# Delta-rule stage of a two-block model: two chains over tile pairs become four chains over single tiles

## The chip, the cores and the metric

The kernel runs on one NeuronCore of one Trainium2 chip. The metric is the device time of one execution in microseconds (us). Three executions of the kernel before took 3952.75, 3956.01 and 3965.37 us; the median is 3956.01 us. The engines are TensorE (PE; its weight loads are shown apart as PEld), VectorE (DVE), ScalarE (ACT), GpSimd (POOL) and SyncE (SP), which issues the DMAs.

## The reference, cut to what matters

The reference is a block of mixers and experts followed by a second block. Only one piece of it is touched here, the RWKV-7 scan of the first block. For each of 8 heads of width 64, for each of two directions of time (forward and reverse), over 256 context tokens and then 1024 latent tokens:

```python
def step(s, inp):
    r_t, w_t, k_t, v_t, a_t, b_t = inp
    sa = einsum('bhvk,bhk->bhv', s, a_t)
    s = s * w_t[:, :, None, :] + sa[..., None] * b_t[:, :, None, :] + v_t[..., None] * k_t[:, :, None, :]
    y = einsum('bhvk,bhk->bhv', s, r_t) if emit else None
```

The outputs of both directions are added, normalized over each head's 64 values (mean, variance, square root), scaled and shifted by `lnx_g` and `lnx_b`, and then `(yn + bonus) * gate` goes to the array `mix`. Everything is float32.

## The kernel before

The kernel is a row of stages with a barrier between them: modulation, the first projection (`project_first`), `rwkv_mix`, `hgrn_mix`, the experts, the second block. Between the barriers each engine runs its own list of instructions in order; semaphores order the engines among themselves. Only `rwkv_mix` (L972 to L1480) is changed, and with it the layout of the arrays in DRAM that it reads.

The stage works in chunks of 64 tokens. Inside one chunk the scan becomes linear algebra: with the products of the keys and queries of the chunk, masked to what comes before (`at`, `cb`, `bkT`, `ck`), one needs the inverse of a unit triangular 64x64 matrix. It is built by doubling: `T` and its transpose `TT` start from blocks of two, and five levels (`w1`, `t1` ... `w5`, `t5`) double the block size. A level multiplies a masked copy `X` of `at` with `T` (step `w`, and VectorE adds the identity to give `W`), and then `TT` with `W` (step `t`, which gives the new `T`). One such problem is a chunk of one head in one direction: 20 chunks x 8 heads x 2 directions = 320 problems. Each is a 64x64 matrix, so four matmuls can stand in the four quadrants (64 rows x 64 columns) of the 128x128 array.

Two chains (`u` = 0, 1) go side by side. Each owns four banks of PSUM. A unit of a chain is one group of 128 channels (two heads) and two tiles of 128 tokens, in both directions: 16 problems. A chain makes 10 units, 5 for its first group of channels and 5 for its second; the 20 units of both chains make the stage. A unit is cut into steps:

- `turn`: 16 transposes of a, b, k and v (L1185); the copies go to ACT (L1298) and DVE (L1353).
- `prodb`, `prodk`: products of b and k with a and r (L1199), which DVE masks (L1346).
- `zed`: masked product with v (L1211). `t0`: `T` from `TT` by products with the identity (L1162).
- POOL makes the first `TT` by three masked multiplications and the addition of the identity (L1445, L1456), and the five `X` (L1441).
- `w` and `t` (L1162): each level also makes the turned inverse `TT` by 16 matmuls of its own, copied by DVE (L1370, L1374).
- `wup` (L1172): inverse times a and times the masked values; `mn` (L1237, L1243, L1244): per chunk a matrix `m` and an addend `n`, so that the state goes through four short steps `c0` to `c3` (L1269, L1399), each `S = m S * tot + n`.
- `intra`, `query`, `inter` (L1252, L1253, L1260, L1280): the outputs, added up in `yacc` (L1409), of both directions.
- After a group's fifth unit the whole of `yacc` (128x1024) is normalized: `mean`, `square`, `var`, `root`, `norm`, `back`, `gate` (L1416 to L1432, L1319, L1323, L1286, L1328, L1474, L1476), and stored (L1143).

The order on each engine is written out by one loop (`interleaved`): for each round `s`, for each chain `u`, it emits the step number `s - OFFSET*u` of that chain, with `OFFSET` 11. An engine that waits for one chain's step holds back the steps of the others that stand behind it in its list.

SP loads a unit two units ahead (L1129 to L1132, 12 DMAs for a unit). Before its first work ACT waits for the two small loads of `lnx` (semaphore `once`, L1118 and L1119, the first DMAs of the stage).

## Time and profile before

| | us |
|---|---|
| median of three runs | 3956.01 |
| span of the profiled execution | 3941.6 |
| median less that span (before the first and after the last instruction, and run to run) | 14.4 |
| first DMA of the stage changed, from the span's start | 771.72 |
| first DMA of the next stage | 1358.74 |
| the stage changed | 587.0 |
| PE busy in it | 441.89 |
| DVE, ACT, POOL busy in it | 316.05, 135.19, 224.26 |

Busy time of a matmul includes the time in which it runs through the array, so a busy PE is not PE at its peak. A group with a small mean can be many short instructions at close distance. The distance from the start of one instruction to the start of the next says more of an engine's rate than the duration of one. The mean granted clock of TensorE was 0.933 over the span. The page's own chain of waits reaches back only to 3743.91 us, into the last projection; it says nothing of the stage changed.

### The profile page before, as it was taken

The numbers are of one execution on the slowest core, as the hardware profiler recorded it, in microseconds if no ns is written. First come the engines' busy times: TensorE is split into PE (matmuls) and PEld (weight loads), VectorE is DVE, ScalarE is ACT, GpSimd is POOL, SyncE is SP. The second block draws the span as 40 slices with busy tenths as digits, with TensorE's granted clock in tenths as the row PEclk, the third lists the DMA queues.
The fourth block names the chain that finished last, engine by engine and source line by source line (L and its number), as shares of the span: only waits on it lengthen the run. The fifth ranks groups of instructions, "written<-read, shape, count | busy, mean of one in ns | idle before, by whom it ended". The sixth has DMA issues, their size and how long they took to land. (4 is left out here: it accounts for less than half of the span.)

```text
span 3941.6 us, 97846 instructions
## 1 busy us (share of the span) xinstructions
PE 3377.2 (86%) x38463; PEld 2331.6 (59%) x38463; DVE 2360.6 (60%) x4245; ACT 1768.8 (45%) x2361; POOL 731.1 (19%) x706
## 2 busy tenths in 40 slices
PE   4999799677778587979998998999689999878789
PEld 0899788577677475733332333333267777666567
DVE  1688688655555466627776766776377574056631
ACT  0577577422222124307776766776222321156620
POOL 4000000043444200331221221222112333200000
PEclk7999899899899788989999999999899999988899
DMA  8354445421221255949889999953734323265452
GB/s 315 84 171 139 160 130 166 159 86 46 61 72 44 82 167 200 209 155 315 277 263 356 351 354 357 326 160 76 244 87 128 86 75 96 95 153 132 117 181 75
DMA packets 520291, 665.36 MB, mean 169 GB/s; under 512 B 77168, under 2 KB 423984, under 8 KB 516768
## 3 DMA queue, kind: packets, MB, share of 16 engines
q1 hardware_dynamic: 494576, 572.44, 45.2%
q0 software_dynamic: 25216, 86.62, 8.9%
q8 instruction: 312, 5.11, 0.5%
q14 instruction: 139, 1.14, 0.1%
q10 hardware_dynamic: 48, 0.05, 0.0%
HBM read 493.08 MB, written 165.94 MB: 167 GB/s over the span
## 5 line engine op out<-in xcount | busy, mean ns | idle before, releaser
L2600 PE MATMUL routed_p_gu<-routed_fixed,routed_x 128*32 128x512 f32 x3840 | 572.5, 600 | 0.0
L2600 PE MATMUL routed_p_gu<-moe_exp_w,routed_x 128*32 x1280 | 571.5, 600 | 0.7 <-DVE routed_fixed L2722 0.7
L2654 ACT COPY routed_fixed<-moe_exp_w 128x1024 f32 x320 | 332.6, 1047 | 222.1 <-DMA moe_exp_w<-in_exp_w_up_dram 86.3
L2722 DVE COPY routed_fixed<-moe_exp_w 128x1024 f32 x640 | 398.0, 681 | 51.3 <-DMA moe_exp_w<-in_exp_w_up_dram 42.9
L544 PE MATMUL front_ps<-front_a_high,front_w_high 128*128 128x320 f32 (+1 forms) x1120 | 362.7, 324 | 16.3 <-DVE front_w_low L797 13.4
L544 PE MATMUL front_ps<-front_a_low,front_w_high 128*128 128x320 f32 (+1 forms) x1120 | 353.8, 316 | 0.0
L544 PE MATMUL front_ps<-front_a_high,front_w_low 128*128 128x320 f32 (+1 forms) x1120 | 353.7, 316 | 0.0
L2600 PEld LDWEIGHTS routed_p_gu<-moe_exp_w,routed_x 128*32 128x32 f32 x1280 | 135.4, 111 | 356.2 <-issue 356.2
L3606 PE MATMUL pre_ps<-pre_a_high,pre_w_high 128*128 128x512 f32 x720 | 287.1, 399 | 13.3 <-ACT pre_xb L3753 6.7
L2615 PE MATMUL routed_p_y<-routed_wd,routed_hT 128*32 x640 | 290.4, 597 | 3.4 <-ACT routed_fixed L2665 3.4
L2615 PE MATMUL routed_p_y<-routed_fixed,routed_hT 128*32 128x512 f32 x1920 | 291.4, 597 | 0.0
L2734 DVE COPY routed_fixed<-routed_wd 128x1024 f32 x320 | 201.7, 691 | 141.2 <-PE routed_p_gu L2600 126.8
L3606 PE MATMUL pre_ps<-pre_a_high,pre_w_low 128*128 128x512 f32 x720 | 281.3, 391 | 0.0
L3606 PE MATMUL pre_ps<-pre_a_low,pre_w_high 128*128 128x512 f32 x720 | 281.2, 391 | 0.0
L2557 POOL DMA_INDIRECT total<-rw_mask,routed_yidx x80 | 128.6, 1608 | 732.2 <-ACT rw_mask L2671 604.6
L544 PEld LDWEIGHTS front_ps<-front_a_high,front_w_high 128*128 128x128 f32 x1120 | 213.3, 190 | 35.2 <-DVE front_w_low L797 18.0
L1445 POOL TENSOR_TENSOR rwmix_TT<-rwmix_at,rw_mask 64x256 f32<-64x256 f32 (+1 forms) x60 | 43.5, 725 | 922.4 <-DVE rwmix_at L1346 916.5
L544 PEld LDWEIGHTS front_ps<-front_a_low,front_w_high 128*128 128x128 f32 x1120 | 213.2, 190 | 1.3
L544 PEld LDWEIGHTS front_ps<-front_a_high,front_w_low 128*128 128x128 f32 x1120 | 213.0, 190 | 0.0
L2665 ACT COPY routed_fixed<-routed_wd 128x1024 f32 x160 | 167.1, 1047 | 47.4 <-PE routed_p_gu L2600 46.7
L2615 PEld LDWEIGHTS routed_p_y<-routed_wd,routed_hT 128*32 128x32 f32 x640 | 70.8, 111 | 196.9 <-issue 196.9
L3606 PEld LDWEIGHTS pre_ps<-pre_a_high,pre_w_high 128*128 128x128 f32 x720 | 135.9, 189 | 46.7 <-issue 16.5
(550 smaller groups left out, 7386.6 us busy)
## 6 DMA issues: line engine op xcount, KB each, us to landing
moe_exp_w<-in_exp_w_gate_dram SPq DMA_DIRECT2D x64, 1024.0 KB, 13.3
moe_exp_w<-in_exp_w_up_dram SPq DMA_DIRECT2D x64, 1024.0 KB, 16.4
routed_wd<-in_exp_w_down_dram SPq DMA_DIRECT2D x64, 1024.0 KB, 15.1
front_wt<-in_w_in_dram SPq DMA_DIRECT2D x70, 512.0 KB, 4.4
mod_w<-in_w_mod_dram SPq DMA_DIRECT2D x24, 1024.0 KB, 18.2
pre_wt<-in_w_in_dram SPq DMA_DIRECT2D x44, 512.0 KB, 4.0
out_a<-mix SPq DMA_DIRECT2D x24, 512.0 KB, 4.0
total<-out_none SPq DMA_DIRECT2D x24, 512.0 KB
```

Source lines behind the costliest of these rows:

```text
L544: op = nc.tensor.matmul(ps[:, s % 2, c, 0:size], w_part[:, s % 2, k, :], a_part[:, k, first + c * size:first + (c + 1) * size], start=(k = ...
L1445: nc.gpsimd.tensor_tensor(combos(TT[u][:])[to, es], combos(at[u][:])[at_rows, es], mask(MASK_LEVEL, at_rows, es), ALU.mult)
L2557: nc.gpsimd.indirect_dma_start(total, bass.IndirectOffsetOnAxis(ap=yidx[b % 2][:, :], axis=0), y[:, b % 2, :], None, compute_op=ALU.add).t ...
L2600: op = nc.tensor.matmul(p_gu[spot(s), :], x[:, b % 2, k, spot(s)], w, start=(k == 0), stop=(k == KD - 1))
L2615: op = nc.tensor.matmul(p_y[spot(s), h, :], hT[:, m, spot(s)], w, start=(m == 0), stop=(m == MT - 1))
L2654: nc.scalar.copy(fixed[:, place_of(b, c), 0, :], wgu[:, bass.ds(e % WS, 1), c * D:(c + 1) * D].rearrange("p o n -> p (o n)"))\
L2665: nc.scalar.copy(fixed[:, at, 0, :], wd[:, bass.ds(e % WD, 1), m, :].rearrange("p o n -> p (o n)"))\
L2722: op = nc.vector.tensor_copy(fixed[:, place_of(b, c), s - 1, :], wgu[:, bass.ds(es[s] % WS, 1), c * D:(c + 1) * D].rearrange("p o n -> p ( ...
L2734: op = nc.vector.tensor_copy(fixed[:, at, s - 1, :], wd[:, bass.ds(e % WD, 1), m, :].rearrange("p o n -> p (o n)"))
L3606: op = nc.tensor.matmul(ps[:, u, a:a + n], w_part[:, u, k, :], a_part[:, k, a:a + n], start=(k == 0 and j == 0), stop=(k == KD - 1 and j = ...
```

## The change

The stage is written anew on the same mathematics:

- Four chains instead of two, one for each group of 128 channels (`GROUPS = QT` = 4), each with two banks of PSUM. A unit is one tile of each direction (8 problems); each chain makes 10 units (`TILES`), then one round of finishing steps. `OFFSET` is 5.
- The inverse: the turned inverse `TT` of a level comes from two full 128x128 transposes of `T` (`turned_inverse`), copied by ACT, instead of from 16 matmuls. The problems lie so that a `w` step crosses from chunk rows to head rows and a `t` step back.
- The state enters ahead of the inverse: `rest` = a S + zed (`as`), new values = inverse times `rest` (`vn`), new state from both parts in one 128-row matmul (`st`). So `wup`, `mn`, `m`, `n`, `q`, `query` and the transposes of a are gone. Each of the two chunk steps is `as`, `vn`, `st`.
- The outputs are made at the end of the second chunk step: eight 128-row matmuls, then eight of 64 rows with the state.
- `lay` and `masked` are rounds with nothing on PE: `lay` is four copies on ACT, `masked` four operations on DVE.
- The decay of the state, `faded`, is made on POOL (two 128x64 operations for each chunk step).
- The normalization is made tile by tile, between the steps of the units after the seventh, and once more at the end.
- Loads: 10 DMAs for a unit (k and v by halves of 64 columns), 400 in all; `tot` is loaded once for all. ACT, DVE and POOL wait at their start for four small loads (`once` >= 64), which SP issues behind the 40 loads of the first units.

The core of the diff:

```diff
-    PAIRS = TILES // 2
-    UNITS = 2 * PAIRS
+    GROUPS = QT
+    LAST = TILES - 1
-    OFFSET = 11
+    OFFSET = 5
-        ps = [st.psum(f"ps{u}", [P, 4, BANK]) for u in range(2)]
+        ps = [st.psum(f"ps{u}", [P, 2, BANK]) for u in range(GROUPS)]
         def slots(n):
+            norm = ["mean", "square", "var", "root", "norm", "back", "res", "gate"] if finishing(n) else []
+            if n == TILES:
+                return norm
+            out = ["turn", "lay", "prod", "masked", "t0"] + norm[0:1]
             for l in range(1, LEVELS + 1):
+                out += [f"w{l}"] + norm[2 * l - 1:2 * l] + [f"t{l}"] + norm[2 * l:2 * l + 1]
+            return out + ["as0", "vn0", "st0", "as1", "vn1"] + (["st1"] if latent(n) or n < LAST else [])
+        def freed(eng, n, u):
+            if n >= 0:
+                DV.wait(eng, by_vector[u], n, "y" if latent(n) else "st1")
# SP
+            for u in range(GROUPS):
+                load(0, u)
+            for d in range(2):
+                sp.dma_start(tot[:, :, d, :], rw["tot"][d].rearrange("(u p) c -> p u c", p=P)).then_inc(once, 16)
             sp.dma_start(lnx[:, 0, :], column(par["lnx_g"])).then_inc(once, 16)
             sp.dma_start(lnx[:, 1, :], column(par["lnx_b"])).then_inc(once, 16)
# PE
+                def turned_inverse():
+                    for e in range(2):
+                        op = nc.tensor.transpose(b[:, 0, span(TT_AT + e * P, P)], T[u][:, 2 * e:2 * e + 2, :], consts["ident"][:, :])
                 if p == "turn":
+                    freed(pe, n - 1, u)
+                    for bank, first, rows in ((0, 0, x[:, B]), (1, 0, kv[u][:, z, K]), (1, 2 * P, kv[u][:, z, V])):
+                        for d in range(2):
+                            op = nc.tensor.transpose(b[:, bank, span(first + d * P, P)], rows[:, d], consts["ident"][:, :])
+                elif p[0] == "w":
+                    AC.wait(pe, by_scalar[u], n, "res" if l == 4 and finishing(n) else f"t{l - 1}")
+                    if l > 1:
+                        turned_inverse()
+                    PO.wait(pe, by_pool[u], n, f"x{l}")
# ACT
+            act.wait_ge(once, 64)
+                elif p == "lay":
+                    stack(bk, 1, 0, 1)
+                    stack(uv, 1, 2 * P, 1).then_inc(by_scalar[u], 1)
# DVE
+                elif p[:2] == "st":
+                    PE.wait(dve, products[u], n, p)
+                    if s == 0 or n < LAST:
+                        PO.wait(dve, by_pool[u], n, f"faded{s}")
# POOL
+                if p == "prod":
                     DV.wait(pool, by_vector[u], n, "at")
+                    for h in range(2):
+                        for c in range(2):
+                            first_level(c, h)
+                    nc.gpsimd.tensor_tensor(TT[u][:].rearrange("p e c t -> p (e c) t"), TT[u][:].rearrange("p e c t -> p (e c) t"), eye4, ALU.add)\
+                        .then_inc(by_pool[u], 1)
                     for l in range(1, 4):
+                        level(l)
                 elif p in ("w1", "w2"):
+                    level(int(p[1]) + 3)
+                elif p[:2] == "as":
+                    if s == 0 or n < LAST:
+                        for d in range(2):
+                            op = nc.gpsimd.tensor_tensor(faded[u][:, s, d, :], S[u][:, z, s, d, :],
+                                                         tot[:, u, d, a:a + 1].broadcast_to([P, HEAD]), ALU.mult)
```

## Rows read from the trace of the kernel before

**Rows 1.** Busy time by stretch: us, instructions, granted clock, DMA share, GB/s.
```profile
771.70:1358.70 587.00, 441.89 (x17088) 401.79 (x17088) 316.05 (x672) 135.19 (x233) 224.26 (x204) 0.94 0.21 59
781.00:1336.00 555.00, 438.96 (x17048) 399.39 (x17047) 308.69 (x662) 132.47 (x229) 215.66 (x201) 0.96 0.20 58
```

**Rows 2.** Timeline of the stage's start: start us, us, engine, line, operation, count.
```profile
771.72 0.38 SPq L1118 DMA_DIRECT2D rwmix_lnx<-in_rw_lnx_g_dram  x1
...
777.31 0.43 SPq L1129 DMA_DIRECT2D rwmix_src<-rw_k  x1
777.79 0.43 SPq L1130 DMA_DIRECT2D rwmix_src<-rw_v  x1
...
781.94 0.59 ACT L1298 COPY rwmix_az<-rwmix_ps 128x512 f32<-128x512 f32 x1 [24.74 <-PE rwmix_ps L1185]
...
784.33 1.74 PEld L1199 LDWEIGHTS rwmix_ps<-rwmix_src 64*64 64x64 f32 x64 [0.33 <-ACT rwmix_kT L1298]
...
785.50 0.69 DVE L1346 TENSOR_TENSOR rwmix_at<-rwmix_ps,rw_mask 128x512 f32<-128x512 f32 x1 [2.08 <-PE rwmix_ps L1199]
786.11 0.68 DVE L1346 TENSOR_TENSOR rwmix_cb<-rwmix_ps,rw_mask 128x512 f32<-128x512 f32 x1
...
786.45 2.45 POOL L1445 TENSOR_TENSOR rwmix_TT<-rwmix_at,rw_mask 128x256 f32<-128x256 f32 x3 [724.09 <-DVE rwmix_at L1346]
...
790.26 4.96 POOL L1441 TENSOR_TENSOR rwmix_X<-rwmix_at,rw_mask 128x512 f32<-128x512 f32 x4
```

**Rows 3.** Timeline of a stretch at full clock.
```profile
877.10 0.56 PEld L1162 LDWEIGHTS rwmix_ps<-rwmix_W,rwmix_TT 64*64 64x64 f32 x32 [0.33 <-DVE rwmix_W L1362]
...
877.56 0.56 PEld L1162 LDWEIGHTS rwmix_ps<-rwmix_TT,rwmix_W 64*64 64x64 f32 x32
...
878.19 0.64 PEld L1185 LDWEIGHTS rwmix_ps<-ident,rwmix_src 128*128 128x128 f32 x6
...
879.33 1.12 PEld L1185 LDWEIGHTS rwmix_ps<-ident,rwmix_src 128*128 128x128 f32 x10 [0.50 <-issue]
...
880.61 0.56 PEld L1162 LDWEIGHTS rwmix_ps<-rwmix_T,rwmix_X 64*64 64x64 f32 x32 [0.17 <-issue]
...
885.89 1.06 PEld L1211 LDWEIGHTS rwmix_ps<-rwmix_vT,rwmix_bkT 64*64 64x64 f32 x32
```

**Rows 4.** Groups by shape: busy us, mean ns of one, idle time before.
```profile
L1441 POOL TENSOR_TENSOR rwmix_X<-rwmix_at,rw_mask 128x512 f32<-128x512 f32 x100 | 126.4, 1283 | 66.1 <-PE rwmix_ps L1162 66.1
L1445 POOL TENSOR_TENSOR rwmix_TT<-rwmix_at,rw_mask 64x256 f32<-64x256 f32 x40 | 28.9, 723 | 5.7
L1370 DVE COPY rwmix_TT<-rwmix_ps 128x256 f32<-128x256 f32 x160 | 60.4, 419 | 92.1 <-PE rwmix_ps L1162 91.9
L2695 ACT COPY routed_hT<-routed_p_h 128x256 f32<-128x256 f32 x80 | 29.1, 363 | 3.4 <-PE routed_p_h L2630 3.4
L2997 ACT COPY attn_pT<-attn_pt 128x128 f32<-128x128 f32 x16 | 4.3, 270 | 1.8 <-PE attn_pt L2961 1.8
L1399 DVE SCALAR_TENSOR_TENSOR rwmix_S<-rwmix_ps,rwmix_tot,rwmix_n 128x64 f32<-128x64 f32 x152 | 35.6, 276 | 7.9 <-PE rwmix_ps L1269 7.9
```

**Rows 5.** Waits of PE in this stage: us in total, times, longest.
```profile
PE rwmix_ps L1162 <- DVE rwmix_W L1362: 31.8, 52, 2.0
...
PE rwmix_ps L1162 <- issue: 20.0, 25, 2.7
```

**Rows 6.** Busy time and granted clock in short stretches, early and late in the stage.
```profile
790.00:800.00 10.00, 5.77 (x300) 5.04 (x304) 3.59 (x7) 1.76 (x3) 6.49 (x6) 1.00 0.59 164
...
1309.00:1312.00 3.00, 1.54 (x73) 1.30 (x69) 1.88 (x6) 0.52 (x1) 0.00 (x0) 1.00 0.00 0
...
1315.00:1318.00 3.00, 1.58 (x53) 1.44 (x57) 1.85 (x2) 0.00 (x0) 0.00 (x0) 0.81 0.03 5
1318.00:1321.00 3.00, 1.93 (x68) 1.64 (x63) 2.85 (x7) 1.64 (x2) 0.00 (x0) 0.63 0.00 0
```

**Rows 7.** Timeline of the stage's end.
```profile
1336.84 0.75 DVE L1409 TENSOR_TENSOR rwmix_yacc<-rwmix_ps,rwmix_yi 128x256 f32<-128x256 f32 x2 [0.83 <-PE rwmix_ps L1280]
...
1358.74 0.37 SPq L1561 DMA_DIRECT2D hgmix_src<-hg_kh  x1
```

More of the change, by code:

```diff
@@ new lines, in each @@
+            return [st.sb(f"{name}{u}", shape) for u in range(GROUPS)]
+        src, kv = each("src", [P, 2, 3, 2, P]), each("kv", [P, 2, 2, 2, P])
+        bk, uv = each("bk", [P, 2, 2, P]), each("uv", [P, 2, 2, P])
+        at, bkT = each("at", [P, 4, HEAD]), each("bkT", [P, 4, HEAD])
+        cc = each("cc", [P, 2, 2, 2, HEAD])
+        T, TT, W = each("T", [P, 4, HEAD]), each("TT", [P, 2, 2, HEAD]), each("W", [P, 2, 2, HEAD])
+        X = each("X", [P, 3, 4, HEAD])
+        zed, rest = each("zed", [P, 2, 2, HEAD]), each("rest", [P, 2, HEAD])
@@ L1060, in rwkv_mix @@
-        PE, DV, AC, PO = (Counts(UNITS, f) for f in (pe_steps, dve_steps, act_steps, pool_steps))
-        order = [(n, p) for n in range(UNITS) for p in slots(n)]
+            norm = ["square", "root", "res"] if finishing(n) else []
+            if n == TILES:
+                return norm
+            out = ["turn", "lay", "t0"]
+            for l in range(1, LEVELS + 1):
+                out += ([f"tt{l}"] if l > 1 else []) + (norm[l - 1:l] if l < 3 else []) + [f"t{l}"] + (norm[2:3] if l == 3 else [])
@@ L1062, in rwkv_mix @@
+            return out + ["vn0", "vn1"]
+        def pool_steps(n):
+            gate = ["gate"] if finishing(n) else []
+            if n == TILES:
+                return gate
+            return ["tt"] + [f"x{l}" for l in range(1, LEVELS + 1)] + gate + ["faded0"] + (["faded1"] if n < LAST else [])
+        PE, DV, AC, PO = (Counts(TILES + 1, f) for f in (pe_steps, dve_steps, act_steps, pool_steps))
+        order = [(n, p) for n in range(TILES + 1) for p in slots(n)]
         block = st.block()
@@ new lines, in tile_of, with latent_columns, problems @@
+        def tile_of(n, d):
+            if d == 0:
+                return n
+            return CTX_TILES - 1 - n if n < CTX_TILES else TILES + CTX_TILES - 1 - n
+        def latent_columns(n, d):
+            a = (tile_of(n, d) - CTX_TILES) * P
+            return slice(a, a + P)
+        def chunk_of(step, d):
+            return step if d == 0 else 1 - step
+        def problems(steps=(0, 1)):
+            return [(s, d, chunk_of(s, d), h) for s in steps for h in range(2) for d in range(2)]
@@ L1144, in _ @@
-            for u in range(2):
-                sp.wait_ge(stored[u], 32)
+            for n in range(1, TILES + 3):
+                for u in range(GROUPS):
+                    if second(n - 3):
+                        store(n - 3, u)
+                    if n < TILES:
+                        load(n, u)
+                    if second(n - 1) and n - 1 < TILES:
+                        load_gates(n - 1, u)
+            for u in range(GROUPS):
+                sp.wait_ge(stored[u], 32 * (LAT_TILES // 2))
@@ new lines, in body @@
+                    if l > 1:
+                        AC.wait(pe, by_scalar[u], n, f"tt{l}")
+                    for e in range(2):
+                        for c in range(2):
+                            for h in range(2):
+                                old, step = TT[u][half(h), e, c, :], W[u][half(h), c, e, :]
+                                if l == LEVELS:
+                                    old, step = step, old
+                                op = nc.tensor.matmul(b[half(c), h, span(T_AT + e * HEAD, HEAD)], old, step, start=True, stop=True)
@@ new lines, in heads, with product, strict @@
+                    return ap.rearrange("p h e v -> p (h e) v")
+                def product(rows, c, side):
+                    v = b[rows, :, span(2 * P * c, 2 * P)].rearrange("p h (e j t) -> p h e j t", e=2, j=2)
+                    return v[:, :, :, side, :]
+                def strict(out, other):
+                    for c in range(2):
+                        rows = half(1 - c if other else c)
+                        op = nc.vector.tensor_tensor(out[u][rows].rearrange("p (e h) t -> p h e t", h=2), product(rows, c, 0),
+                                                     mask(MASK_AFTER)[rows].rearrange("p e h t -> p h e t"), ALU.mult)
+                    op.then_inc(by_vector[u], 1)
```

580 lines of the change are left out of this document (233 added, 347 removed).

## Prediction

> **What bounds the kernel now.** I read the busy time by stretch first, then the timeline of the stage's two ends, then the groups by shape. Barriers stand on both sides of the stage, so only its length counts: 587.0 us from its first DMA to the next stage's first [rows 1, 2, 7]. PE is busy in 442 of them, and the steady part, from the first transposes (781) to the last outputs (1336), is 555 us, that is 55.5 us for each of the ten pairs of units. No engine is full: PE waits, most of it (31.8 us on the biggest line) for DVE [rows 5].
>
> **Engine work after the change.** First the prices, then whether an engine becomes the bound.
>
> - PE. A 64-column float32 matmul shows as two records. With all four quadrants in use 16 of them issue in 0.46 us (877.10 to 877.56), 0.029 each; with two quadrants (L1211) about 0.055; 128-column products 32 in 1.74, 0.054 each [rows 2, 3]. A full transpose takes 1.12/10 = 0.11. The end of a step lies 0.2 us behind its last issue. A chain's tile after the change: turn 6 x 0.11 = 0.66, prod 16 x 0.054 = 0.87, t0 0.22, w1 0.23, four w steps at 0.22 + 0.23, five t steps at 0.23, zed 0.45, as and vn 2 x (0.12 + 0.22), st 2 x 0.32, outputs 0.45 + 0.23: 7.4 us, 40 times, 296.
> - POOL. 256 elements take 0.723, 512 take 1.283 [rows 4]: 2.2 ns an element and 0.17 fixed, so a 64x128 operation should take 0.45, a 128x64 one 0.31. Three first-level operations of 0.725 take 2.45 with their drains [rows 2]: 0.14 between two; without a drain neighbours overlap by 0.04 (four X of 512 elements in 4.96). The first TT: 4 x 0.59 + 0.73 = 3.1. Three X at 0.68: 2.05. Two more X 1.4, two faded pairs 1.2. 7.8 us a tile, 310 in all (224 now), plus 24 for gates.
> - ACT. 256 elements take 0.363, 128 take 0.270 [rows 4], and neighbours overlap by about 0.1. Eight 64x256 copies, ten of 128x256, four of 128 columns: 6.9 a tile, 276 in all (135 now).
> - DVE. Twelve operations of 256 elements at 0.42 (0.335 when queued, by the 0.61 from 785.50 to 786.11 for 0.69 long ones [rows 2]), two of 128 elements near 0.29, four at 0.24: 5.8 a tile, 232 (316 now) plus about 37 of normalization.
>
> PE loses 100 us or more, ACT and POOL gain about 140 and 110, none comes above 340 of 587. So the length is set by the order in which the engines wait.
>
> **The loop that I think sets the pace.** With OFFSET 5 and 21 steps a unit, the next chain's `turn` comes five rounds after this one's, and its old unit's `as1` falls into the same round as this one's `prod`, behind it (for the last chain one round later). Let zero be the moment at which DVE has finished `at` of chain A; B is the chain behind it.
>
> 1. POOL starts 0.2 later (786.19 to 786.45 [rows 2]), TT is done at 3.3, the three X at 5.4, and only then come B's `faded1` pair: 6.0. POOL takes them in order.
> 2. On PE, `t0` of A waits for TT until 3.4; B's `st1` and the outputs stand behind it (issue 3.6 to 4.6, done 4.8). They are not last: DVE holds B's `st1` for `faded1` until 6.1. State pair 0.47 and output copy: 6.9. DVE's `rest` of one chain and W1 of A are queued behind this.
> 3. B's `turn` waits for that output (`freed`): PE 6.95, done 7.8. Behind it on PE, until 8.95, come vn0 of a third chain, w4 of a fourth and t1 of A, which waited for the same DVE.
> 4. ACT: two `bk` copies of B, two of vn0, one of w4, then `zed` twice and T1 of A (their product is done at 9.15), and only then `lay` of B: four copies, done at 11.1.
> 5. `prod` of B: 16 matmuls and the tail, 12.25; DVE makes `at`: 13.1. The loop closes.
>
> So 13.1 us for each tile of each chain, in which PE issues 7.4 us. To this I add 0.35 for changes between full and quartered use of PE: 16 matmuls that issue in 0.46 end their issue at 878.02 and transposes start at 878.19; the transposes' issue ends at 880.45 and the quartered ones start at 880.61 [rows 3], 0.1 to 0.17 each, three on the loop. Another 0.35 for stops of PE that show as "issue" (20.0 us in 25 of them on the biggest line [rows 5]; I take twice that for all lines, 40, less by the fall of PE's instructions from 17,088 pairs [rows 1] to about 12,300, half of it on the loop: 14 over 40 windows). Taken: 13.8 us.
>
> The Trainium skill, TensorEngine Tiling (Array Packing), section Tiling Modes, says that changing the tiling mode drains TensorE. By that rule the two 128x128 transposes inside every w step are worse than they look; the trace agrees with the 0.1 to 0.17 us just given.
>
> **The sum.**
> - Start. SP issues a DMA every 0.48 us (777.31, 777.79 [rows 2]). The four loads that ACT, DVE and POOL wait for are behind 40 others: 44 x 0.48 = 21, and I allow 6 for their landing behind 7168 short packets; ACT begins at about 799 instead of 781.94. bk, lay, prod and at bring the first zero to 803: 31 us into the stage.
> - The first three windows have no `faded1` of an older unit before them. Their loop is t0 (3.4), T, w1, `turn`, t1, `lay`, `prod`, `at`: 10.1 each, 30.
> - The other 36 windows of the 39 between 40 `at`s: 36 x 13.8 = 497.
> - Normalization: 8 more rounds in units 7, 8 and 9. Between the last chain's `at` and the first chain's next lie 14 rounds instead of 6; at about 1.6 us a round 23 instead of 13. Twice: 20.
> - Drain, from the last `at`: TT and t0 4.3, levels 13, their normalization 3, six state steps 7.5, the final steps 9.5 with the store, 4 for chains ahead: 41. Now it takes 22 us from the last output (1336.84) to the next stage (1358.74) [rows 7], after it perhaps 12; this gain is inside the 41.
> - Barrier and next issue: 1.5.
>
> Sum 621 against 587: 34 us more. Span 3941.6 + 34 = 3976; with the 14.4 between that span and the median, 3990.
>
> **Bounds.** Not shown before: a 64x128 operation on POOL. From below 0.27 (nothing on POOL's groups of two inputs is that short), from above 0.725: the loop is 0.7 shorter or 1.1 longer. The ACT queue between bk and lay: if t1's copies are not ahead of lay, the loop is 1.6 shorter; that is the largest favourable bound. Wait on DMA: loads are issued a whole unit (50 us) ahead, so nothing; from above a stop of a few us at the first units. Switches and stops: 0 to 1.4. Start: once lands between 795 and 806. Loop 10.8 to 16, so 3880 to 4070.
>
> **Rivals.**
> - A, faster. The chains don't close into the loop: `faded1` of B gets ahead of its need, because PE's `st1` is later than I think or POOL's X are quicker, and `lay` isn't held by t1. Then the pace is the first windows' 10.1 to 12: at 12.0, 36 x 1.8 = 65 us less, 3925; at 10.1, 3857. It decides from the point where POOL's block (now 5.4) ends before PE's `st1` (4.8). For it: every engine has 40% or more to spare, and 0.6 us separates the two. Against: even then t0 holds PE until 3.4.
> - B, slower: the clock. PE would issue in 7.4 of 13.8 us, with gaps of about 1.8 us at t0 and at `turn`. In the steady part the clock is 0.96 at 79% busy [rows 1], but where PE fell to 1.54 us in 3 the clock came down to 0.81 and 0.63 in the next stretches [rows 6], between its levels 2.4 and 1.2 GHz. If it stays low, PE needs 14.8 us a window and the loop about 17: 36 x 3.2 = 115 more, 4105. Half of that time low: 4045. Against: a slow PE is a busy PE, and the stretch from 790 to 800, 58% busy, was at the full clock [rows 6]. The Trainium skill, TensorE: Matmul & The Clock Gate, section "A second HAM failure mode: psum-queue depth-cycling", says that a PE which is idle for short moments between groups swings between both levels; rows 6 agree with it.
> - C, no change: a loop of 12.9 and everything else as said. 3950 to 3968.
>
> **How the numbers follow.** The loop as worked (12.9 to 15): 0.52, its own range 3960 to 4035. A 0.28, B 0.14, C 0.06. 3990 is the forecast; the range that leaves two in ten outside is 3885 to 4065. Within 0.3% (12 us, what three runs can tell from no change) lies C and an edge of the others, 0.08; faster 0.30, slower 0.62.
>
> **What would show it.** In the stage after: ACT's first copy near 799; 40 `at` about 13.8 us apart, the first three about 10; before DVE's `st1` an idle time that POOL's `faded` ends, about 1.2 us each; PE's `t0` ended by POOL's TT; POOL busy 330, ACT 280, PE 330 to 370; clock 0.9 or more. I am wrong if the distance of two `at` is under 12.5, if `faded` ends hardly any wait, or if the clock is under 0.85.

## The result and the profile after

| | before | after |
|---|---|---|
| median of four runs each, us | 3954.38 (3948.32 to 3965.37) | 4028.09 (4023.37 to 4030.05) |
| ratio, 95% interval | | 1.0191, 1.0164 to 1.0218 |
| span of the profiled execution | 3941.6 | 4027.4 |
| first DMA of the stage changed | 771.7 | 776.1 |
| first work of the next stage | 1358.7 | 1438.8 |
| stage changed | 587.0 | 662.7 |

The change makes the kernel slower by 74 us. Of the 86 us between the two spans 76 lie in the stage, 4 ahead of it and 6 behind it; the profiled execution of the kernel before was a quick one (12.8 us under its median, that of the kernel after 0.7), so the medians are closer to each other than the spans. The forecast was 3990: right in direction and inside its range, but less than half of the loss. One of the six runs of the last kernel in the table of experiments, 4010.62 us, fell in a slower state, at a mean clock of 0.85; its median 3915.05 counts that run, its ratio does not.

The start of the stage is this row:

```profile
776.09 0.37 SPq L1124 DMA_DIRECT2D rwmix_src<-rw_abrk  x1
```

A window, below, is the time from POOL's first operation on the `TT` of one unit to the same operation of the next unit, which belongs to the next chain: the prediction's loop once round. There are 39 of them. The first eleven or so make no outputs (context tokens), and what follows the last one is called the drain.

Busy time by stretch of the kernel after (length, then busy us of PE, PE's loads, DVE, ACT and POOL, granted clock, DMA share, GB/s, as in [rows 1]): 771.7 to 1432, then four windows with outputs, three context windows, and two stretches of the drain.

```profile
771.70:1432.00 660.30, 469.56 (x11904) 368.54 (x11904) 270.20 (x789) 314.09 (x929) 300.38 (x583) 0.87 0.21 52
981.00:1038.00 57.00, 41.73 (x1219) 32.81 (x1216) 24.44 (x72) 29.47 (x88) 27.99 (x56) 1.00 0.20 49
843.50:890.50 47.00, 35.44 (x820) 27.62 (x816) 17.45 (x52) 22.17 (x67) 20.97 (x42) 0.82 0.18 44
1384.00:1398.00 14.00, 10.81 (x271) 8.35 (x270) 7.18 (x19) 6.88 (x21) 9.50 (x16) 0.78 0.07 21
1412.00:1432.00 20.00, 12.05 (x242) 8.42 (x240) 9.39 (x28) 7.79 (x23) 6.54 (x11) 0.76 0.10 28
```

PE has 5184 fewer matmul records than before [rows 1], and the stage is longer. No engine is full, as before. The mean clock is 0.87 against 0.94 before: 1.00 in the four windows with outputs, 0.82 in the three context windows, under 0.8 in the two stretches of the drain.

The waits of the stage, of DVE and PE (us in total, times, longest):

```profile
DVE rwmix_W L1373 <- ACT rwmix_TT L1305: 189.2, 145, 5.5
DVE rwmix_S L1387 <- POOL rwmix_faded L1455: 69.8, 25, 3.1
PE rwmix_ps L1195 <- POOL rwmix_TT L1439: 57.9, 39, 4.6
...
PE rwmix_ps L1187 <- ACT rwmix_uv L1290: 45.4, 40, 17.7
...
PEld rwmix_ps L1207 <- issue: 30.0, 158, 0.3
```

PE's wait for DVE's W, its longest before [rows 5], is down to 7.0 us. In its place stand the two waits that steps 1 and 2 named, `t0` for POOL's TT and DVE's `st1` for `faded`, and `prod` for ACT's `lay`. POOL's `faded` ended 25 of DVE's waits before a new state; 11 others (31.4 us) ended with PE's outputs. The largest row, DVE's W for ACT's copy of TT, is not what sets the pace, as far as these runs show: from 850 to 1250 it is 138.2 us here and still 132.7 us in the kernel of the last experiment, whose windows are 2.4 us shorter.

One turn of the loop, from the timeline (PE's weight loads, `prod`'s single records and some others left out). The `turn` of one chain starts at 1002.01 and that of the next at 1016.51.

```profile
1002.01 0.41 PE L1178 MATMUL rwmix_ps<-ident,rwmix_src 128*128 128x128 f32 x2 [1.23 <-DVE rwmix_yacc L1395]
...
1004.05 0.63 PE L1224 MATMUL rwmix_ps<-rwmix_uv,rwmix_bkT 64*64 64x64 f32 x16
...
1004.74 0.74 ACT L1310 COPY rwmix_zed<-rwmix_ps 64x256 f32<-64x256 f32 x2 [0.15 <-PE rwmix_ps L1224]
...
1005.76 0.74 ACT L1290 COPY rwmix_bk<-rwmix_ps 64x256 f32<-64x256 f32 x2
...
1006.52 0.74 ACT L1290 COPY rwmix_uv<-rwmix_ps 64x256 f32<-64x256 f32 x2
...
1008.49 0.86 DVE L1356 TENSOR_TENSOR rwmix_at<-rwmix_ps,rw_mask 64x256 f32<-64x256 f32 x2
...
1009.52 0.45 POOL L1429 TENSOR_TENSOR rwmix_TT<-rwmix_at,rw_mask 64x128 f32<-64x128 f32 x1 [1.93 <-DVE rwmix_at L1356]
...
1012.86 2.10 POOL L1424 TENSOR_TENSOR rwmix_X<-rwmix_at,rw_mask 128x256 f32<-128x256 f32 x3
1013.05 0.41 PE L1195 MATMUL rwmix_ps<-ident,rwmix_TT 128*128 128x128 f32 x2 [1.52 <-POOL rwmix_TT L1439]
...
1013.67 0.64 PE L1256 MATMUL rwmix_ps<-rwmix_uv,rwmix_cc 128*64 128x64 f32 x16
1014.24 0.46 PE L1261 MATMUL rwmix_ps<-rwmix_S,rwmix_src 64*64 64x64 f32 x16
...
1014.92 1.04 POOL L1455 TENSOR_TENSOR rwmix_faded<-rwmix_S,rwmix_tot 128x64 f32<-128x64 f32 x4
...
1015.56 0.47 DVE L1387 SCALAR_TENSOR_TENSOR rwmix_S<-rwmix_ps,rwmix_tot,rwmix_faded 128x64 f32<-128x64 f32 x2 [3.06 <-POOL rwmix_faded L1455]
...
1015.96 0.41 DVE L1395 COPY rwmix_yacc<-rwmix_ps 128x256 f32<-128x256 f32 x1
...
1016.51 0.41 PE L1178 MATMUL rwmix_ps<-ident,rwmix_src 128*128 128x128 f32 x2 [1.23 <-DVE rwmix_yacc L1395]
```

Read it as the prediction's loop, with zero at 1009.35 where DVE ends `at`: TT done 3.5, X done 5.6, DVE's `st1` begins 6.2, the output is copied at 7.0, `turn` 7.2. The idle of 3.06 us on DVE ends when POOL has made `faded`, behind the three X. From the first `turn` the circle closes over `zed`, `lay` and `at` to the next TT, 7.3 us from that `turn` to the end of `at` where the prediction had 6.15.

The group rows that answer to [rows 4], by shape:

```profile
L1429 POOL TENSOR_TENSOR rwmix_TT<-rwmix_at,rw_mask 64x128 f32<-64x128 f32 x160 | 72.1, 451 | 861.0 <-DVE rwmix_at L1356 843.6 <-issue 0.4
L1290 ACT COPY rwmix_bk<-rwmix_ps 64x256 f32<-64x256 f32 x160 | 58.6, 366 | 103.5 <-PE rwmix_ps L1178 64.7 <-DMA rwmix_lnx<-in_rw_lnx_b_dram 37.7
L1455 POOL TENSOR_TENSOR rwmix_faded<-rwmix_S,rwmix_tot 128x64 f32<-128x64 f32 x152 | 39.9, 294 | 2.9 <-DVE rwmix_S L1387 2.9
```

A 64x128 operation on POOL takes 0.451 (0.45 was estimated), a 128x64 one 0.294 (0.31).

### The profile page after: what moved, and what is told of

It reads as the page before. It is cut to its first block and busy times, and to the rows that moved or that the text cites. A ratio compares the mean times of both kernels' runs of the same rounds, so it can differ in the third digit from the quotient of the medians.

```text
span 4027.4 us, 89389 instructions
## 1 busy us (share of the span) xinstructions
PE 3407.8 (85%) x33279; PEld 2302.3 (57%) x33279; DVE 2316.6 (58%) x4362; ACT 1946.6 (48%) x3057; POOL 806.9 (20%) x1086
## 5 line engine op out<-in xcount | busy, mean ns | idle before, releaser
L544 PE MATMUL front_ps<-front_a_high,front_w_high 128*128 128x320 f32 (+1 forms) x1120 | 364.5, 325 | 16.4 <-DVE front_w_low L797 13.4
L1429 POOL TENSOR_TENSOR rwmix_TT<-rwmix_at,rw_mask 64x128 f32<-64x128 f32 x160 | 72.1, 451 | 861.0 <-DVE rwmix_at L1356 843.6
L1373 DVE TENSOR_TENSOR rwmix_W<-rwmix_ps,eye 128x256 f32<-128x256 f32 x200 | 84.1, 422 | 200.1 <-ACT rwmix_TT L1305 189.2
```

The lines of the kernel that those rows point to most:

```text
L544: op = nc.tensor.matmul(ps[:, s % 2, c, 0:size], w_part[:, s % 2, k, :], a_part[:, k, first + c * size:first + (c + 1) * size], start=(k = ...
L1373: nc.vector.tensor_tensor(W[u][:].rearrange("p c e t -> p c (e t)"), both_banks(b, W_AT, 1), eye4.rearrange("p (c e) t -> p c e t", c=2), ...
L1429: nc.gpsimd.tensor_tensor(TT[u][half(h), :, c, :], at[u][half(c), h::2, :], consts["rw_mask"][half(c), MASK_LEVEL, h::2, :], ALU.mult)
```

## The experiments

"Window" is a mean over four neighbouring windows with outputs, which takes in all four chains once. "Next" is when the next stage starts in the profile, "stage" the time to it from the stage's own first DMA, which came between 772.2 and 776.7 in these profiles. Ratios are to the kernel before, on the same chip; (one) marks a kernel that ran once, which has no ratio.

| kernel | median us | ratio, 95% | next | stage | window |
|---|---|---|---|---|---|
| after | 4028.09 | 1.0164 to 1.0218 | 1438.8 | 662.7 | 14.35 |
| faded1 a round earlier | 3989.94 | 1.0083 to 1.0138 | 1412.5 | 638.0 | 13.4 to 13.8 |
| `once` loads first | 4012.33 | 1.0144 to 1.0198 | 1424.2 | 651.3 | 14.35 |
| `lay` in the round of `turn` | 4038.92 (one) | | 1456.3 | 683.6 | 15.2 |
| `lay` by half | 4016.58 (one) | | 1425.1 | 650.9 | 14.0 to 14.2 |
| the three edits (without `lay` in `turn`) | 3973.57 | 1.0033 to 1.0072 | 1389.0 | 616.8 | 13.5 to 13.9 |
| the three and a third empty round | 3890.84 | 0.9820 to 0.9873 | 1302.0 | 528.8 | 11.6 |
| faded1 earlier, outputs mixed | 4181.25 (one) | | 1594.5 | 821.8 | 20.0 |
| no empty rounds | 4078.47 (one) | | 1492.2 | 719.0 | 15.3 to 16.2 |
| third empty round alone | 4010.77 | 1.0148 to 1.0196 | 1428.1 | 651.4 | 14.5 |
| OFFSET 4 | 3964.60 | 1.0034 to 1.0074 | 1377.6 | 603.0 | 12.5 |
| the three, OFFSET 4 | 3945.31 | 0.9986 to 1.0020 | 1355.5 | 581.3 | 12.4 |
| outputs in context too (second time) | 4015.78 | 1.0132 to 1.0207 | 1427.3 | 654.4 | 14.35 |
| faded1 earlier and third empty round | 3915.05 | 0.9876 to 0.9939 | 1332.1 | 557.5 | 11.9 |

**Is faded1 on the loop?**

```diff
-                elif p[:2] == "as":
-                    s = int(p[2])
+                elif p in ("as0", "st0"):
+                    s = 0 if p == "as0" else 1
```

> Changed: POOL makes the decayed state of the second chunk step (faded1) in the round of st0 instead of as1, so it no longer stands behind the next-older chain's block of TT and three X. Nothing is left out. Loop theory (the tiles follow each other at the pace of one closed chain of waits, of which POOL's block is a part): DVE's st1 then waits for PE's st1 only, about 0.8 us earlier (PE's part ends near 1014.7, DVE began at 1015.56), so the distance between two first-TT operations falls from 14.2-14.6 to about 13.6 us and the stage by about 29 us. Rival, PE theory (PE is busy 38 of 50 us, the tiles follow at its pace and waits only fill its gaps): the distance stays at 14.4 and the stage within 5 us.

Most of the windows with outputs fell from 14.2 to 14.6 to 13.4 us, the stage by 24.7 us. In this kernel's timeline DVE's `st1` is ended by PE, not by POOL, and after 1.98 us instead of 3.06:

```profile
1040.52 0.47 DVE L1387 SCALAR_TENSOR_TENSOR rwmix_S<-rwmix_ps,rwmix_tot,rwmix_faded 128x64 f32<-128x64 f32 x2 [1.98 <-PE rwmix_ps L1261]
```

So `faded1` was on the loop. What comes late next is PE's `st1`, 0.8 us earlier, because it stands behind `t0`.

**The loads that everybody waits for.**

```diff
-            for u in range(GROUPS):
-                load(0, u)
...
+            for u in range(GROUPS):
+                load(0, u)
```

> Changed: the four small loads for which ACT, DVE and POOL wait at their start are issued ahead of the forty loads of the first units instead of behind them. Nothing is left out. Theory (the start is lost to the order of SP's queue): ACT's first copy comes at about 782-784 instead of 799.3 us, and the stage is 16 us shorter (forty issues of 0.48 us are 19). Rival (the forty loads themselves land late, or the later chains arrive no earlier, since each waits for its own loads and five rounds): ACT starts early but the fourth chain's first tile comes when it came before, and the stage is under 5 us shorter.

The first TT starts at 788.6 instead of 804.9. The stage itself began 3.2 us earlier in this profile, so from its own start the first TT comes after 15.8 us instead of 28.9. The stage is 11.4 us shorter, with the windows with outputs unchanged and the first three 3.3 us longer together. That lies between the theory (16) and its rival (under 5). The wait for the small loads is a cost of the start alone.

**Is ACT's `lay` late because it is emitted late?**

```diff
                     stack(bk, 0, 0, 0).then_inc(by_scalar[u], 1)
-                elif p == "lay":
                     stack(bk, 1, 0, 1)
```

> Changed: ACT makes the four copies of lay in the round of turn, directly behind the two bk copies, instead of a round later behind vn0, w4 and zed and T1 of the other chains. PE and DVE keep their order. Nothing is left out. Loop theory: lay ends about 2.1 us earlier (six copies of 0.37 from the end of the transposes, 1017.4 to 1019.6, against 1021.8), and prod with it; other chains' T1 is later but not in the chain of waits: distance 14.4 to 12.4-13, stage 50 to 70 us shorter. PE theory: distance and stage as before, within 5 us. Third way: the 1.5 us later vn0, tt4 and T1 take lay's place in the chain and eat half the gain: distance 13.5.

It went the other way, to 15.2 us. The timeline shows the shared queue: `lay` (the last two of the four copies from 1048.00, behind `turn`'s own two, and the two from 1049.53) is done early, but vn's copy comes behind it at 1050.30, PE's `st0` waits 1.09 us for that, and `zed` comes after both.

```profile
1048.00 1.51 ACT L1290 COPY rwmix_bk<-rwmix_ps 64x256 f32<-64x256 f32 x4 [1.92 <-PE rwmix_ps L1178]
...
1049.53 0.74 ACT L1290 COPY rwmix_uv<-rwmix_ps 64x256 f32<-64x256 f32 x2
1050.30 0.53 ACT L1316 COPY rwmix_uv<-rwmix_ps 64x128 f32<-64x128 f32 x2
1050.85 0.37 ACT L1304 COPY rwmix_TT<-rwmix_ps 128x256 f32<-128x256 f32 x1
1050.88 0.46 PE L1249 MATMUL rwmix_ps<-rwmix_uv,rwmix_bk 128*64 128x64 f32 x8 [1.09 <-ACT rwmix_uv L1316]
1051.12 0.74 ACT L1309 COPY rwmix_zed<-rwmix_ps 64x256 f32<-64x256 f32 x2
```

PE has those steps ahead of `prod`, so `prod` comes 5.8 us behind its `turn` (1047.12 to 1052.95) instead of 5.3 (1002.01 to 1007.31), although its data are there from 1050.27.

**Do ACT's copies overlap?**

```diff
-                    stack(bk, 1, 0, 1)
-                    stack(uv, 1, 2 * P, 1).then_inc(by_scalar[u], 1)
+                    for side in range(2):
+                        stack(bk, 1, 0, 1, (side,))
+                        op = stack(uv, 1, 2 * P, 1, (side,))
+                    op.then_inc(by_scalar[u], 1)
```

> Changed: only the order of the four lay copies on ACT: k and v of partitions 0 to 63, then k and v of 64 to 127, instead of k of both halves and then v of both. Nothing is left out. In the trace two neighbouring copies of different halves start 0.37 us apart at a duration of 0.366, while a 128-partition copy before another start 0.27 apart. Theory (the overlap of neighbours is lost when the next writes other partitions): two of three changes of half go, four copies last 1.28 instead of 1.48 us, distance 0.2 shorter, stage 8 us shorter. Rival (copies of 64 partitions from one bank never overlap): four copies stay at 1.48 us and the stage is the same.

```profile
1053.31 0.36 ACT L1290 COPY rwmix_bk<-rwmix_ps 64x256 f32<-64x256 f32 x1
1053.57 0.37 ACT L1290 COPY rwmix_uv<-rwmix_ps 64x256 f32<-64x256 f32 x1
1053.95 0.37 ACT L1290 COPY rwmix_bk<-rwmix_ps 64x256 f32<-64x256 f32 x1
1054.23 0.37 ACT L1290 COPY rwmix_uv<-rwmix_ps 64x256 f32<-64x256 f32 x1
```

Neighbours on the same half start 0.26 and 0.28 apart, neighbours on different halves 0.38, which is their full length. In the kernel after each pair in `lay` changes halves, two copies in 0.74 us. The four copies now last 1.29 us instead of about 1.5, and the windows with outputs are 0.3 us shorter, which is the theory. Of the 11.8 us that the stage lost, 8.3 came in the eight context windows; the last five of them ran at full clock (see below).

**The three edits together.**

> The three edits that shortened the stage one by one are put together: faded1 of the earlier chain a round earlier on POOL (alone -26 us of stage), the small loads of once ahead of the 40 loads of the tiles (alone -14.6 us), and ACT's four lay copies ordered by half of the partitions (alone -13.7 us). Nothing of the computation is left out. Theory L (each edit takes time out of another link of one loop that runs from window to window, and the loads out of the start, so the gains add): stage 667 less 26, 15 and 13 = about 613, distance of the first TT's in the latent windows 13.1, time before plus 25 to 32 us, ratio 1.007. Theory P (once faded1 is out of the way TensorE's own work of a window, not the loop, sets the distance, so copies saved on ACT give nothing more): distance stays 13.4, stage about 626, ratio 1.0105. In both cases it is slower than the kernel before.

The stage fell by 45.9 us against 47.9 for the sum of the three, close to theory L; but the windows with outputs stayed near 13.6, as theory P had it. Against the kernel with faded1 alone, what is gained beyond the start came in the eight context windows, 100.8 us instead of 109.7.

**A third empty round on top.**

```diff
-            out = ["turn", "lay", "prod", "masked", "t0"] + norm[0:1]
+            out = ["turn", "lay", "prod", "masked", "hold", "t0"] + norm[0:1]
```

> As the kernel with the three edits, and one more empty round between masked and t0 (22 steps to a tile instead of 21), so that TensorE emits st1 and the outputs of the chain behind ahead of t0, which waits for POOL's first TT. Nothing of the computation is left out. Theory W (TensorE's stop of 1.2 to 1.5 us for TT at t0 stands on the loop, with st1, y and the next turn behind it): the distance falls by 0.8 to 1.5 us, to about 12, and the stage by 30 to 55 us, which would bring the time level with the kernel before or below it. Rival R (the windows are made of rounds that cost about the same, 5.25 of them to a window, now 5.5): the distance rises by 0.3 to 0.65 us, stage plus 12 to 26 us. Rival N (t0's wait is replaced by an equal one for the turn of the next chain, which now stands behind t0): within 0.2 us of the distance.

More than theory W expected: 88 us of stage for one round. This is the fastest kernel of the study, 1.5% faster than the one before (ratio 0.9846, 0.9820 to 0.9873). Three windows take 10.0 to 10.7 us and the fourth 14.7 to 16.1.

**What grouping the outputs is worth.** Based on the kernel with faded1 earlier.

```diff
                             opened.add((c, h))
-                        for s, d, c, h in problems():
-                            y = b[half(c), h, span(Y_AT + (d if second(n) else 1 - d) * HEAD, HEAD)]
...
```

> On top of faded1 a round earlier (distance 13.4 us in latent windows, next stage at 1412.5 us): the outputs not grouped by kind, each problem's product with the 128-row uv followed at once by its product with the 64-row state. Nothing of the computation is left out. Price of one change between a 128-row and a 64-row matmul by the rows: 0.1 to 0.17 us more than inside one kind; 15 changes instead of 1 make 1.4 to 2.4 us. Theory S (TensorE's outputs stand on the loop, ahead of y and of the next turn): the distance in the 32 latent windows rises by 1.4 to 2.4 us, to 14.8 to 15.8, the stage by 45 to 75 us; the context windows stay. Rival H (the change of kind costs nothing when both kinds are queued): under 0.3 us. Rival O (it costs, but off the loop): output matmuls take longer and the distance stays at 13.4.

Theory S, at three times its price: 20.0 us instead of 13.4. The outputs on PE, first at half clock (granted 0.54 from 1034 to 1040), later at full clock (1.00 from 1053.5 to 1055):

```profile
1036.00 0.47 PE L1256 MATMUL rwmix_ps<-rwmix_uv,rwmix_cc 128*64 128x64 f32 x2
1036.40 0.47 PE L1259 MATMUL rwmix_ps<-rwmix_S,rwmix_src 64*64 64x64 f32 x2
...
1053.62 0.28 PE L1256 MATMUL rwmix_ps<-rwmix_uv,rwmix_cc 128*64 128x64 f32 x2
1053.84 0.33 PE L1259 MATMUL rwmix_ps<-rwmix_S,rwmix_src 64*64 64x64 f32 x2
1054.09 0.33 PE L1256 MATMUL rwmix_ps<-rwmix_uv,rwmix_cc 128*64 128x64 f32 x2
```

A mixed product takes 0.22 to 0.25 us at the full clock, a grouped one 0.07 (eight in 0.57 us, 1013.67 to 1014.24 in the kernel after): 0.15 to 0.18 for each change of kind, and at half clock 0.40 in all. The clock came down too: it was 0.76 from 1000 to 1100 against 0.98 in the kernel with only faded1 moved, so that everything else on PE took longer. An estimate from these rows: sixteen mixed products at 0.25 us take some 3 us more than grouped ones at full clock, so the rest of the 6.6 us goes with the low clock; the one run of this kernel does not part them further. In it the stage is 184 us longer than with the outputs grouped.

**Without the empty rounds.**

```diff
-            out = ["turn", "lay", "prod", "masked", "t0"] + norm[0:1]
+            out = ["turn", "prod", "t0"] + norm[0:1]
```

> The kernel after without its two empty rounds: lay is copied in the round of turn and the masks bk and cc are made in the round of prod, so a tile has 19 steps instead of 21. Nothing of the computation is left out. Theory Q (queues in order: what stands right behind a long chain of dependences waits with it): TensorE's prod then waits in the next round for ACT's six copies, and t0 waits in the round after prod for DVE's at and POOL's 3.3 us of first TT, with only one round of other chains' steps between, so the distance rises by 1 to 3 us, stage plus 40 to 120 us. Rival R (the distance goes by the number of rounds, 4.75 instead of 5.25 for a window): distance 14.4 falls to about 13.0, stage minus 50 us.

Theory Q: 15.3 to 16.2 us. PE waits longer for TT at `t0`, as this row of its timeline shows (1.52 us in the kernel after):

```profile
1038.14 0.41 PE L1195 MATMUL rwmix_ps<-ident,rwmix_TT 128*128 128x128 f32 x2 [3.11 <-POOL rwmix_TT L1437]
```

**The third round by itself.** The edit as above, on the kernel after.

> The kernel after, with a third empty round between masked and t0 and nothing else changed: 22 steps to a tile instead of 21, nothing of the computation left out. It parts what the round did in the kernel that had the three edits too. Theory C (two coincidences of rounds made the loop of the kernel after: faded1 of the chain behind stood behind POOL's first TT, and st1 with its outputs stood on TensorE behind t0, which waits for that TT; one more round parts both): distance 10 to 11 us for three windows and about 15 for the fourth, mean 11.7, as with the three edits (11.5), stage shorter than that of the kernel after by 95 to 115 us, next stage at 1325 to 1345, time 3915 to 3935, ratio to before 0.990 to 0.995. Rival F (the round pays only once faded1 is moved and ACT's copies are ordered by half): mean distance 13 or more, next stage after 1390, slower than before.

My theory C fell. I had miscounted: the round parts `st1` from `t0`, but not `faded1` from POOL's block. Chain B is five rounds behind A. With 21 steps its `as1` (step 18) meets A's step 18+5-21=2, `prod`; with 22 it is step 19 and meets 19+5-22=2, `prod` again. The timeline says so:

```profile
1043.29 0.48 DVE L1387 SCALAR_TENSOR_TENSOR rwmix_S<-rwmix_ps,rwmix_tot,rwmix_faded 128x64 f32<-128x64 f32 x2 [2.71 <-POOL rwmix_faded L1455]
...
1044.24 0.66 PE L1178 MATMUL rwmix_ps<-ident,rwmix_src 128*128 128x128 f32 x2 [2.21 <-DVE rwmix_yacc L1395]
```

PE's wait for TT is gone and its wait at `turn` has grown from 1.23 to 2.21. After that wait PE's records are at half clock (0.66 instead of 0.41).

The round does pay at once where no `faded1` is made yet. The first three windows took 10.7, 11.0 and 10.2 us instead of 12.9, 13.7 and 12.0, although PE's mean clock over the three was no higher (0.75 against 0.80). The third window of each kernel, the kernel after first, is at full clock in both:

```profile
831.49:843.53 12.04, 9.07 (x256) 6.99 (x256) 5.37 (x15) 6.75 (x21) 6.49 (x12) 1.00 0.01 3
```

```profile
827.20:837.38 10.18, 8.37 (x238) 6.46 (x234) 4.71 (x13) 6.90 (x20) 6.46 (x12) 1.00 0.01 3
```

What the round moves there is B's `turn`, which now stands on PE ahead of A's w1 instead of behind it, and B's `lay`, which stands on ACT ahead of the copies of A's t1.

**Other coincidences, same number of rounds.**

```diff
-    OFFSET = 5
+    OFFSET = 4
```

> The kernel after with OFFSET 4 instead of 5 and nothing else: 21 steps to a tile, the chains 4, 4, 4 and 9 rounds apart instead of 5, 5, 5 and 6; nothing left out. faded1 then comes a round ahead of the next chain's first TT on POOL, and st1 a round ahead of its t0. Theory C (it is these two coincidences, not the number of rounds): three windows of 8 to 9 us and one of 19 or so, mean 11 to 12, next stage at 1320 to 1350, ratio 0.988 to 0.997. Rival E (even spacing of the chains is what matters; with 4, 4, 4, 9 the first three stand in each other's way on ACT and DVE, and the last leaves TensorE idle and its clock low): mean distance 13 to 14.5, next stage at 1390 to 1440.

> The three edits (faded1 a round earlier, the once loads first, lay copies by half) with OFFSET 4 and without an extra round; nothing left out. Theory C with rounds of equal cost (46.0 us for 22 rounds of four windows in the kernel with three edits and an extra round is 2.09 us a round, so 21 rounds would take 44): mean distance 11.0, next stage at about 1285, ratio 0.980 to 0.984. Rival E (uneven spacing costs more than the round saved): mean 12 or more, next stage after 1320. Rival B (by now the engines' own work sets the rate, TensorE 88 of 100 us busy at full clock): mean distance stays 11.5, next stage at 1302, the same time as with the extra round.

Three windows take 9.8 to 10.4 us, a little less than with the extra round. The fourth, nine rounds long, takes 19.2 to 20.1 in the steady part, and the two that hold the normalization 33.3 to 34.2. The first expectation fell between its two theories, in the second rival E held: parting the coincidences gains, uneven spacing gives part of it back.

**Is the low clock of the context windows a cost?**

```diff
-                    if s == 1 and latent(n):
+                    if s == 1:
```

> The kernel after, with the 16 matmuls of the outputs (32 records of a window) issued in the context windows too, where nobody reads them; all else as it is. In the kernel after the context windows ran at a clock of 0.82 with a distance of 15.3 to 15.9 us, the latent ones with the outputs at 0.94 to 1.00 with 14.2 to 14.6. Theory K (TensorE's low activity without the outputs lets the clock fall, and the low clock is the whole difference): clock 0.94 or more in the context windows and a distance of 14.2 to 14.6 although TensorE has more work; stage 5 to 12 us shorter. Rival T (the difference has another cause and the added 1.2 us of matmuls comes on top): 15.5 to 17 us, stage up to 10 us longer. Rival U (the clock state varies from run to run by itself, as the kernel with ordered lay copies had 13.7 us at clock 1.00 in the same windows without the outputs): either, with no relation to the edit; then one look can't tell.

> The same kernel as the one look before: the kernel after with the output matmuls issued in the eight context windows too, where nobody reads them. Theory K (they keep the clock up and the clock made these windows longer): context windows at 13.9 to 14.4 us again, median time 4010 to 4018, below the 4023 to 4030 us that the kernel after took in its runs. Rival U (chance): median 4022 to 4032, and the context windows anywhere between 13.9 and 15.9.

The stretch 850 to 930 in this kernel (second run) and in the kernel after:

```profile
850.00:930.00 80.00, 61.23 (x1747) 48.22 (x1749) 33.94 (x98) 43.25 (x130) 39.34 (x78) 0.98 0.20 49
```

```profile
850.00:930.00 80.00, 60.89 (x1380) 47.30 (x1384) 29.36 (x86) 38.16 (x114) 35.31 (x71) 0.82 0.18 45
```

Six of the eight context windows took 13.9 us in both profiles of this kernel, 14.6 to 15.9 in the kernel after, and the eight together 112 instead of 123 us, with more matmuls issued. Theory K held: at the higher clock these windows are 11 us shorter. In the whole time the gain is not clear of noise: the medians (4012.25, 4015.78) agree, but the intervals of the two ratios overlap. Nor are the added matmuls the only way to the full clock. The kernel with `lay` by half makes no outputs there, and its last five context windows took 13.7 us each at full clock, with PE busy for a smaller share of the time:

```profile
900.00:959.00 59.00, 42.69 (x1204) 32.92 (x1202) 25.64 (x74) 31.41 (x97) 29.66 (x59) 1.00 0.19 48
```

So the low clock is the cost, as shown twice; that it is low because PE is idle without the outputs is not shown.

**Both waits, nothing else.** The edits of the first experiment and of the third round.

> The kernel after with faded1 of the chain behind a round earlier on POOL and the third empty round, and neither the once loads first nor the lay copies by half; nothing left out. Theory V (two waits that end within a microsecond of each other close the same loop: after the round alone DVE still waited 2.7 us for faded1, which still stood behind the next chain's TT and X; after faded1 alone TensorE still waited 1.2 to 1.5 us for TT; only both together open it): mean distance 11.5 to 12.2 us, next stage at 1316 to 1345, time 3905 to 3935. Rival A (ACT's order of copies or the loads carry half of the gain of the four edits together): mean distance 13, next stage at 1365 to 1395, time 3955 to 3985.

Theory V. The two edits alone were worth 25 and 11 us of stage, together they are worth 105, 69 more than the sum. Of its waits these two rows, of the stretch 850 to 1250, answer to PE's wait for TT and DVE's for `faded`, which are 33.9 us in 27 waits and 55.6 us in 20 in the same stretch of the kernel after:

```profile
PE rwmix_ps L1195 <- POOL rwmix_TT L1439: 4.3, 2, 2.2
```

```profile
DVE rwmix_S L1387 <- POOL rwmix_faded L1455: 0.6, 1, 0.6
```

The first window of this kernel shows the third thing that the round moves, as in the kernel with the round alone. `lay` of B now comes one step ahead of A's `t1` instead of behind it: the `uv` copies start at 810.39 and `zed` at 811.62, where the kernel after has `zed` first (1004.74, then 1005.76).

```profile
808.86 1.51 ACT L1290 COPY rwmix_bk<-rwmix_ps 64x256 f32<-64x256 f32 x4 [0.91 <-PE rwmix_ps L1178]
...
810.39 0.74 ACT L1290 COPY rwmix_uv<-rwmix_ps 64x256 f32<-64x256 f32 x2
...
811.62 0.74 ACT L1310 COPY rwmix_zed<-rwmix_ps 64x256 f32<-64x256 f32 x2 [0.49 <-PE rwmix_ps L1224]
```

How these 69 us split between PE's order, ACT's order and the clock was not taken apart. PE's busy share went with it, 89.66 of 100 us (1000 to 1100) at clock 0.97, against 75.72 at the same clock in the kernel after.

## Why the prediction was right, and where it was not

The mechanism of the loop held point by point. The first TT began at 804.94, just behind `at`; in windows with outputs DVE's `st1` waited for `faded` behind X, `t0` for TT, and moving `faded1` took out 0.8 us a window. Rival A (the loop doesn't close) and rival C are refuted. Two of the signs missed: the clock was 0.87 where 0.9 or more was named, and PE was busy 470 us instead of 330 to 370. The sum was 621 us for a stage of 663. Term by term, from the starts of the 40 first TTs (804.94 to 1384.53) and the stage's own start, 776.09:

| term | forecast | measured | off |
|---|---|---|---|
| start, to the first TT | 31 | 28.9 | -2.1 |
| first three windows | 30 | 38.6 | +8.6 |
| eight context windows | 8 x 13.8 = 110.4 | 123.1 | +12.7 |
| 26 other windows | 26 x 13.8 = 358.8 | 364.2 | +5.4 |
| two windows with normalization | 47.6 | 53.7 | +6.1 |
| drain and barrier | 42.5 | 54.3 | +11.8 |

The step that failed is the sum, in its terms outside the steady loop: the first three windows at 10.1 each, the context windows at the price of the loop at full clock, the drain at 41. These three came out 33 of the 42 us too small. I worked out one loop at the full clock and priced the rest by rounds. The loop itself was nearly right: 14.35 in the windows with outputs against 13.8, and 14.0 as a mean of the 26, the last ones being shorter.

- The context windows: the clock. I put rival B aside as a whole (0.14) because the stretch 790 to 800 was at full clock before. It was true in parts: 0.82 in three context windows, 0.78 and 0.76 in the drain. The experiment with outputs in context puts 11 of the 12.7 us on it.
- The first three windows: the order, more than the clock. PE comes out of a 4.56 us wait at half clock, with transposes of 0.69 instead of 0.41, but the third of these windows was at full clock throughout and took 12.0. With a third empty round alone the three took 31.9 us, 1.9 above the forecast, at a mean clock of 0.75 against 0.80 here. So 6.7 of the 8.6 us go with B's `turn` behind w1 and B's `lay` behind t1's copies, an order that I had listed and priced too low.
- The drain: mostly open. It took 51.1 us in the second profile with outputs in context, where the clock was 0.93 (1376 to 1420), against 54.3 here at 0.82 (1384.5 to 1432). That would put some 3 of the 11.8 us on the clock. For the rest, and for the 6.1 us of the windows with normalization, no run shows which step was too small.
- Inside the loop I took the ACT copies as overlapping by 0.1. Copies on different halves don't: step 4, from `t1`'s product to the end of `lay`, took 2.6 us (1004.68 to 1007.26) where 1.95 was taken. The 0.35 for other "issue" stops, of which the turn of the loop shown has none, made up for about half of it. So that the loop came out near 13.8 was in part luck, two errors of opposite sign.
- Changes between full and quartered use of PE were priced a little low: PE's loads wait 30.0 us in 158 times for issue before L1207, 0.19 each, four a window, against 0.1 to 0.17, three on the loop. By the Trainium skill, TensorEngine Tiling (Array Packing), section Tiling Modes, a change of mode drains the engine; the mixed outputs agree, with 0.15 to 0.18 us for each change.
- The favourable bound that I named and didn't follow, "if t1's copies are not ahead of lay", was the door to the faster kernel together with the TT wait. I priced it at 1.6 us. In the first three windows, where the round moves both `turn` and `lay`, it was 1.9 to 2.7 us, and with both waits parted the windows with outputs fell by 2.4 to 2.8.

## What to carry to other kernels

Where chains share in-order queues, write down for every step that waits which steps of the other chains meet it in the same round, for each engine and with the step numbers recounted after every edit; here one empty round and one moved pair of operations were worth 113 us together and turned +1.9% into -0.9%. Two waits that end within a microsecond of each other can hide each other, as here: taking out one showed 25 or 11 us, both together 105. So test both together before giving up on either. Price the clock by stretch, not for the stage as a whole, and work out the start, the drain and stretches with less matmul work by themselves instead of by the steady loop's price.

## What the runs showed of the hardware that was not expected

- ACT copies of 64x256 that follow on the same half of the partitions start 0.26 to 0.28 us apart, on different halves 0.38 us, their full length. DVE shows the same: `at`, two operations on different halves, 0.86 us; `cc`, two of 128x256, 0.74.
- Alternating 128-row and 64-row matmuls costs 0.15 to 0.18 us a change at the full clock, against 0.07 for a grouped 128-row product itself.
- With matmuls added whose result nobody reads, eight windows were 11 us shorter in all, in two profiles, and the clock there was 0.98 instead of 0.82. But the clock also stayed at 1.00 without them, in the kernel with `lay` by half; what decides between the two is not shown.
